# Hybrid trunk kernel: three of a pair's scatter products placed ahead of the jump out of its body, and the second expert's gather placed in the pair's block 0

## The chip, the cores and the metric

The kernel runs on one core of one Trainium2 chip. The metric is the device time of one execution in microseconds; the median of several executions is compared. The engines are PE (TensorE, matrix products), DVE (VectorE), ACT (ScalarE), POOL (GpSimd) and SP (SyncE, which issues the weight loads here).

## What is computed

Two layers of a decoder trunk with 256 tokens of width 1024 in float32. The change lies in the last sub-layer, a routed SwiGLU with eight experts of which each token takes two:

```python
def swiglu(h, w_gate_up, w_down):
    gate, up = jnp.split(h @ w_gate_up, 2, axis=-1)
    return (jax.nn.silu(gate) * up) @ w_down

def moe_swiglu(h, w_router, b_router, w_gate_up, w_down):
    tok = h.reshape(bsz * seq, d)
    probs = jax.nn.softmax(tok @ w_router + b_router, axis=-1)
    top_p, top_i = lax.top_k(probs, TOP_K)             # TOP_K = 2
    top_p = top_p / jnp.sum(top_p, axis=-1, keepdims=True)
    gates = jnp.sum(jax.nn.one_hot(top_i, N_EXPERTS) * top_p[..., None], axis=1)
    out = jnp.zeros_like(tok)
    for e in range(N_EXPERTS):                         # 8 experts, hidden width 3584
        out = out + gates[:, e:e + 1] * swiglu(tok, w_gate_up[e], w_down[e])
```

## The kernel before, in words

**Pairs.** After the router (until about 620 us) the eight experts are handled as four pairs in a loop (Fori over p, lines 2705 for PE, 1863 for DVE, 1074 for ACT). Each engine holds its own copy of the loop and, within it, five bodies, one of which is chosen at run time by the pair's kind through nested branches (expert_pairs, lines 440 to 452). A body is either wide (pair_wide: the first expert has more than 64 tokens and is computed in a split precision, with or without a further tail of 32 tokens) or light (pair_light: both experts have few tokens). In this run pairs 0, 1 and 2 are wide, 0 and 1 with a tail and 2 without one, and pair 3 is light. When a body ends, the engine jumps over the other bodies to what stands behind them, then back to the loop's head, and through the branches into the next body.

**Blocks.** An expert's hidden width is cut into seven blocks f of 512. A block needs three weight granules of 2 MB: gate, up and down. The first expert of a pair is a, the second b, and b runs one block behind a; the granules' order is that of pair_order (ag, au, ag, au, ad, bg, ad, bu, ag, ...). Each granule goes into one of seven ring buffers; SP issues the loads in order, and each waits until the granule seven places earlier was read (`used`).

**One wide block.** PE computes main_gate, main_up, main_turn (transposes of the activated product) and main_down for the 128 main tokens (24 records of 512 columns per granule, line 2227); tail_in, tail_turn and tail_down for the tail (64 records of 128 columns per granule at line 2485, 16 of 512 columns at 2497); and second_in, second_turn and second_down for expert b. ACT rounds each half of a granule (w_round, line 990), DVE forms the rest (w_rest, line 1794), and PE waits for both (`wlo_done`). DVE also multiplies the activations (lines 1800 and 1846) and writes the low part of the turned ones (a3_lo, line 1834), which releases main_down.

**A pair's end (pair_end).** PE: second_in of the last block, next_gather(p + 1) for the next pair's first expert, second_in, second_down of block 5, second_turn and second_down of block 6, and gather_second(p + 1), 32 records of 64 columns (line 2452) into T_BANK that pick the tokens of the next pair's second expert. Then comes the jump out of the body, and behind it scatter_pair, eight matmul calls at lines 2476 and 2477, each two records in the trace, that spread the pair's results over the tokens. ACT and DVE copy the results out of PSUM into ysb4 (lines 948 to 955, 1777, 1781). DVE ends with second_out(p + 1) (lines 1729 and 1733), which scales the gathered tokens of the second expert into xe2 and waits for PE's gather first. For pair 0 the gather and second_out stand ahead of the loop.

**A pair's head.** DVE forms x_lo (line 1811), splits the first halves, computes the scatter weights (weigh_pair), adds the scattered results of the pair before (add_scattered, line 1708) and copies the transposed weights (keep_pair_weights, lines 1760 and 1762), which releases main_up(0). PE's pair_weights transposes those weights into U_BANK and T_BANK; ahead of the second part it waits for `xe2_done`, since T_BANK held the gathered tokens.

## Time and profile before

| | us |
|---|---|
| median of 3 executions | 1584.27 (1583.06 to 1584.80) |
| the profiled execution's own time | 1584.35 |
| its span in the profile | 1582.6 |
| PE busy / DVE busy / ACT busy | 1407.1 / 665.0 / 499.9 |
| mean granted clock of PE | 0.94 |
| DMA, mean over the span | 300 GB/s, 410 GB/s where the queue is full |

Times in the rows are microseconds from the span's start. "issue" in a chain is time in which an engine waited for nothing that the profile shows. A bracket behind a row is the idle time of the engine just before it and what ended it. PEq, PEldq and DVEq are the sequencers, which wait, branch and load registers while their engine is idle or works off its queue.

### The profile page before, as it was taken

How to read it: one execution, taken by the hardware profiler on the slowest of the kernel's cores; microseconds unless marked ns; L12 is line 12 of the kernel's file. 1: busy time of each engine (PE TensorE's matmuls, PEld its weight loads, DVE VectorE, ACT ScalarE, POOL GpSimd, SP SyncE). 2: the span in 40 equal slices, each digit the busy share in tenths (PEclk: the TensorE clock that was granted, in tenths of full speed). 3: DMA queues.
4: the chain of work that ended last, by engine and by line, in shares of the span. 5: the costliest groups of instructions: out<-in, count | busy, mean ns of one | idle time of the engine just before them, and what ended most of it. 6: DMA issues, size and time to landing. Idle time of an engine off the chain costs nothing.

```text
span 1582.6 us, 25911 instructions
## 1 busy us (share of the span) xinstructions
PE 1407.1 (89%) x11147; PEld 995.9 (63%) x11148; DVE 665.0 (42%) x770; ACT 499.9 (32%) x562; POOL 34.8 (2%) x66
## 2 busy tenths in 40 slices
PE   4999999999998798899998899997788887796886
PEld 2763788887784547677675677675566655463443
DVE  5933445454201725755452755451664551100003
ACT  2323543433201512444432544432353431000001
POOL 2001000000100010000000000000000000000000
PEclk9989999999999996999999999999798999798898
DMA  8785875455744034399999699999599999799991
GB/s 301 274 319 207 314 287 202 173 200 176 302 160 159 1 145 174 115 368 412 411 412 410 233 368 412 410 412 410 211 353 412 412 412 409 296 413 411 413 414 75
DMA packets 206823, 474.63 MB, mean 300 GB/s; under 512 B 9986, under 2 KB 10030, under 8 KB 206670
## 3 DMA queue, kind: packets, MB, share of 16 engines
q1 hardware_dynamic: 199968, 470.83, 77.0%
q10 hardware_dynamic: 6702, 1.71, 0.5%
q8 instruction: 103, 1.69, 0.4%
q14 instruction: 50, 0.41, 0.1%
HBM read 471.47 MB, written 1.05 MB: 299 GB/s over the span
## 4 chain that ended last, share of the span: by engine, by line
PE 67%; DMA 12%; SPq 8%; issue 5%; DVE 5%; ACT 2%; DVEq 1%; ACTq 1%; POOL 0%
PE ps L2227 33%; DMA ring<-in_moe_w_down_dram 8%; SPq L488 8%; PE ps L2485 7%; PE ps L2497 5%; PE ps L2310 4%; DMA ring<-in_ada_w_dram 2%; PE ps L2374 2%; PE ps L2203 2%; PE ps L2318 2%; PE ps L2038 1%; PE ps L2452 1%; DMA ring<-in_moe_w_gate_up_dram 1%; DVE ring_lo L1794 1%; PE ps L2102 1%
## 5 line engine op out<-in xcount | busy, mean ns | idle before, releaser
L1794 DVE TENSOR_TENSOR ring_lo<-ring,w 128x2048 fp32r<-128x2048 f32 x126 | 288.3, 2289 | 177.7 <-ACT w L990 148.0
L990 ACT ACTIVATE w<-ring 128x2048 fp32r<-128x2048 f32 x126 | 240.6, 1912 | 242.4 <-PE ps L2227 241.1
L2485 PE MATMUL ps<-ring,arena 128*32 128x128 f32 (+1 forms) x5376 | 255.0, 300 | 40.1 <-DMA ring<-in_moe_w_gate_up_dram 25.6
L2485 PEld LDWEIGHTS ps<-ring,arena 128*32 128x32 f32 (+1 forms) x5376 | 191.3, 117 | 104.0 <-issue 52.1
L2227 PE MATMUL ps<-ring_lo,x_hi 128*128 128x512 f32 x560 | 220.3, 393 | 0.0
L2227 PE MATMUL ps<-w,x_hi 128*128 128x512 f32 x336 | 137.0, 408 | 16.8 <-DVE ring_lo L1794 11.8
L2227 PE MATMUL ps<-w,x_lo 128*128 128x512 f32 x336 | 132.6, 395 | 0.0
L1456 DVE TENSOR_TENSOR ring_lo<-ring,w_hi 128x2048 fp32r<-128x2048 f32 x42 | 95.6, 2290 | 86.1 <-ACT w_hi L766 86.1
L2227 PEld LDWEIGHTS ps<-ring_lo,x_hi 128*128 128x128 f32 x560 | 106.3, 190 | 21.9 <-issue 1.5
L2497 PE MATMUL ps<-ring,tri 128*32 128x512 f32 (+1 forms) x448 | 73.9, 676 | 29.7 <-DMA ring<-in_moe_w_down_dram 28.2
L766 ACT ACTIVATE w_hi<-ring 128x2048 fp32r<-128x2048 f32 x42 | 78.8, 1909 | 50.0 <-PE ps L2227 42.1
L2227 PEld LDWEIGHTS ps<-w,x_hi 128*128 128x128 f32 x336 | 64.2, 191 | 45.8 <-DVE ring_lo L1794 20.9
L2227 PE MATMUL ps<-w_hi,x_hi 128*128 128x512 f32 x224 | 89.4, 399 | 0.0
L2227 PE MATMUL ps<-w_hi,x_lo 128*128 128x512 f32 x224 | 87.4, 390 | 0.0
L2227 PE MATMUL ps<-w,a_hi 128*128 128x512 f32 x168 | 70.1, 417 | 4.5 <-DVE a_lo L1834 4.5
L2227 PEld LDWEIGHTS ps<-w,x_lo 128*128 128x128 f32 x336 | 64.2, 191 | 13.9
L2227 PE MATMUL ps<-ring_lo,a_hi 128*128 128x512 f32 x168 | 67.2, 400 | 0.0
L2227 PE MATMUL ps<-w,a_lo 128*128 128x512 f32 x168 | 67.0, 399 | 0.0
L2038 PE MATMUL ps<-ring,c 128*32 128x512 f32 x384 | 49.2, 664 | 13.3 <-DMA ring<-in_ada_w_dram 13.0
L2497 PEld LDWEIGHTS ps<-ring,tri 128*32 128x32 f32 (+1 forms) x448 | 18.7, 125 | 61.9 <-DMA ring<-in_moe_w_down_dram 31.6
L2310 PE MATMUL ps<-hT,ring 128*128 128x256 f32 x256 | 57.1, 387 | 0.0
L2497 PE MATMUL ps<-ring,arena 128*32 128x512 f32 (+1 forms) x336 | 53.2, 608 | 3.4 <-DVE arena L1708 2.7
(388 smaller groups left out, 1607.4 us busy)
## 6 DMA issues: line engine op xcount, KB each, us to landing
ring<-in_moe_w_gate_up_dram SPq DMA_DIRECT2D x112, 2048.0 KB, 16.7
ring<-in_moe_w_down_dram SPq DMA_DIRECT2D x56, 2048.0 KB, 18.2
ring<-in_ada_w_dram SPq DMA_DIRECT2D x24, 2048.0 KB, 11.0
ring<-in_ffn_w_gate_up_dram SPq DMA_DIRECT2D x14, 2048.0 KB, 12.0
ring<-in_ffn_w_down_dram SPq DMA_DIRECT2D x7, 2048.0 KB, 7.7
ring<-in_sb_w_qkv_dram SPq DMA_DIRECT2D x6, 2048.0 KB, 8.7
ring<-in_s_w_out_dram SPq DMA_DIRECT2D x2, 2048.0 KB, 8.4
ring<-in_sb_w_out_dram SPq DMA_DIRECT2D x2, 2048.0 KB, 13.4
```

What stands on the lines that cost most here:

```text
L488: sp.dma_start(dst, src).then_inc(landed[n % RING], 16)
L766: act.activation(ff_half(w_hi[:, g % 2, :], half).bitcast(F32R), ff_half(gran(ff_place(g)), half), ACT.Copy).then_inc(whi_done, 1)
L990: act.activation(half3(h).bitcast(F32R), ff_half(gran(pair_place(*main_granule(n))), half), ACT.Copy).then_inc(whi_done, 1)
L1456: dve.tensor_tensor(ff_half(ring_lo[(ff_place(g)) % RING][:, :], half).bitcast(F32R), w, ff_half(w_hi[:, g % 2, :], half), ALU.subtract).t ...
L1794: dve.tensor_tensor(ff_half(ring_lo[place % RING][:, :], half).bitcast(F32R), ff_half(gran(place), half), half3(h), ALU.subtract).then_inc ...
L2038: ins = pe.matmul(ps[32 * j:32 * j + 32, ada_bank(i), :], c32[:, 4 * part_k + k, :], gran8(places[r])[:, 4 * part_k + k, :], start=k == 0, ...
L2203: ins = pe.matmul(ps[:, 2 * i + half, :], yT[:, k, P * tt:P * tt + P], gran4(WOUT_PLACES[half])[:, k, 512 * n:512 * n + 512], start=k == 0 ...
L2227: ins = pe.matmul(dst, stationary[a].bitcast(F32R), moving[b].bitcast(F32R), start=start and i == 0, stop=stop and i == 2)
L2310: ins = pe.matmul(ps[:, 2 * (r % 2) + j // 2, 256 * (j % 2):256 * (j % 2) + 256], gran8(n)[:, k, P * j:P * j + P], hT[:, k, :], start=k == ...
L2318: ins = pe.matmul(ps[:, Y_BANK + 2 * tt + r, :], tokens(k, tt), gran8(n)[:, k, :], start=k == 0, stop=k == KD - 1)
L2485: ins = pe.matmul(dst[width * r:width * r + width, 0:cols], x[:, k, 0:width], weights[:, k, cols * r:cols * r + cols], start=k == 0, stop= ...
L2497: ins = pe.matmul(ps[width * r:width * r + width, bank, :], a[:, j, 0:width], weights[:, j, 512 * h:512 * h + 512], start=first and i == 0 ...
```

## The change

Three of the eight calls of scatter_pair, those of the first expert's results for the outputs 0, 1 and 2, go into a new function scatter_first, which PE runs at the end of pair_end, ahead of the jump; they wait for the copies into ysb4 through two new semaphores, first_act and first_dve. The other five calls stay behind the jump. In a light pair one of ACT's copies moves to DVE, so that both semaphores are counted in either kind. gather_second(p) leaves pair_end and the place ahead of the loop; it now stands in block 0 of its own pair, behind main_up(0) (in the light body behind the first up product), and waits for the second `st_done` of that pair. second_out(p) moves on DVE into block 0 too, behind a3_lo (light: behind the first product_first). pair_weights no longer waits for `xe2_done`; the first second_in does.

```diff
--- before.py
+++ after.py
@@ -321,6 +321,7 @@
         xe1_ps, xe1_done = sem("xe1_ps"), sem("xe1_done")
         pick2_done, onehot2_done, xe2_ps, xe2_scaled, xe2_done = (
             sem("pick2_done"), sem("onehot2_done"), sem("xe2_ps"), sem("xe2_scaled"), sem("xe2_done"))
+        first_act, first_dve = sem("first_act"), sem("first_dve")
         n_silu, n_act, n_tr, n_aT = sem("n_silu"), sem("n_act"), sem("n_tr"), sem("n_aT")
 
 
@@ -946,8 +947,8 @@
                 wait_used2(act, p, "ad", FB - 1)
                 if not light:
                     act.activation(ysb4[:, 0, :], ps[:, Y_BANK, :], ACT.Copy)
-                act.activation(ysb4[0:64, 2, :], ps[0:64, Y_BANK + 2, :], ACT.Copy)
-                act.activation(ysb4[64:P, 3, :], ps[64:P, Y_BANK + 2, :], ACT.Copy)
+                    act.activation(ysb4[64:P, 3, :], ps[64:P, Y_BANK + 2, :], ACT.Copy)
+                act.activation(ysb4[0:64, 2, :], ps[0:64, Y_BANK + 2, :], ACT.Copy).then_inc(first_act, 1)
 
             def second_results(p):
 
@@ -1774,12 +1775,14 @@
                 second_selection(p + 1)
                 if not light:
                     wait_used2(dve, p, "ad", FB - 1)
-                    dve.tensor_copy(ysb4[:, 1, :], ps[:, Y_BANK + 1, :])
+                    dve.tensor_copy(ysb4[:, 1, :], ps[:, Y_BANK + 1, :]).then_inc(first_dve, 1)
+                else:
+                    wait_used2(dve, p, "ad", FB - 1)
+                    dve.tensor_copy(ysb4[64:P, 3, :], ps[64:P, Y_BANK + 2, :]).then_inc(first_dve, 1)
                 next_out(p + 1)
                 product_second(p, FB - 1, width)
                 wait_used2(dve, p, "bd", FB - 1)
                 dve.tensor_copy(ysb4[0:64, 3, :], ps[0:64, Y_BANK + 3, :]).then_inc(ysb_dve, 1)
-                second_out(p + 1)
 
             def pair_wide(p, tails, split, tail, width):
 
@@ -1833,6 +1836,8 @@
                     dve.wait_ge(a3_done, split * FB + f + 1)
                     dve.tensor_tensor(a3_lo[:, :, :].rearrange("p k n -> p (k n)").bitcast(F32R), ps[:, G_BANK, :],
                                       a3_hi[:, :, :].rearrange("p k n -> p (k n)"), ALU.subtract).then_inc(m_aT, 1)
+                    if f == 0:
+                        second_out(p)
                     if f < FB - 1:
                         w_rest(2 * n + 6)
                         w_rest(2 * n + 7)
@@ -1852,6 +1857,8 @@
                 keep_pair_weights(p)
                 for f in range(FB):
                     product_first(f)
+                    if f == 0:
+                        second_out(p)
                     if f:
                         product_second(p, f - 1, W2)
                 pair_end(p, W2, True)
@@ -1859,7 +1866,6 @@
             with dve.If(paired(dve) > 0):
                 dve.memset(rt[:, 0, 72:73], 0.0).then_inc(sc_done, 4 * PAIRS)
                 second_selection(0)
-                second_out(0)
                 with nc.Fori(0, PAIRS, engines=[dve.engine], hint_back_edge=True) as p:
                     tails, split, by_kind = expert_pairs(dve, p)
                     by_kind(lambda tail, width: pair_wide(p, tails, split, tail, width), lambda: pair_light(p))
@@ -2447,6 +2453,7 @@
             def gather_second(p):
 
                 pe.wait_ge(onehot2_done, 2 * p + 2)
+                pe.wait_ge(st_done, 2 * p + 3)
                 for k in range(KD):
                     for tt in range(TT):
                         ins = pe.matmul(ps[:, T_BANK, W2 * k:W2 * k + W2], hn[:, tt, P * k:P * k + P], g2[:, tt, :],
@@ -2461,21 +2468,33 @@
                         ins = pe.transpose(ps[:, U_BANK, 256 * i + P * tt:256 * i + P * tt + P],
                                            gw2[:, tt, P * i:P * i + P], ident[:, :])
                 ins.then_inc(st_ps, 1)
-                pe.wait_ge(xe2_done, p + 1)
                 for tt in range(TT):
                     ins = pe.transpose(ps[:, T_BANK, P * tt:P * tt + P], gw2[:, tt, 2 * P:3 * P], ident[:, :])
                 ins.then_inc(st_ps, 1)
 
+            def scattered(i):
+
+                tt, h = divmod(i, 2)
+                return ps[:, Y_BANK + i, :], slice(P * tt, P * tt + P), h
+
+            def scatter_first(p):
+
+                pe.wait_ge(first_act, p + 1)
+                pe.wait_ge(first_dve, p + 1)
+                for i in range(3):
+                    dst, tokens_t, h = scattered(i)
+                    pe.matmul(dst, scT[:, 0, tokens_t], ysb4[:, h, :], start=True, stop=False)
+
             def scatter_pair(p):
 
                 pe.wait_ge(ysb_act, p + 2)
                 pe.wait_ge(ysb_dve, p + 2)
                 for i in range(4):
-                    tt, h = divmod(i, 2)
-                    tokens_t = slice(P * tt, P * tt + P)
-                    pe.matmul(ps[:, Y_BANK + i, :], scT[:, 0, tokens_t], ysb4[:, h, :], start=True, stop=False)
-                    pe.matmul(ps[:, Y_BANK + i, :], (scT2 if h else scT[:, 1, :])[:, tokens_t], ysb4[:, 2 + h, :],
-                              start=False, stop=True).then_inc(sc_ps, 1)
+                    dst, tokens_t, h = scattered(i)
+                    if i == 3:
+                        pe.matmul(dst, scT[:, 0, tokens_t], ysb4[:, h, :], start=True, stop=False)
+                    pe.matmul(dst, (scT2 if h else scT[:, 1, :])[:, tokens_t], ysb4[:, 2 + h, :], start=False, stop=True
+                              ).then_inc(sc_ps, 1)
 
             def shared(dst, x, weights, width):
 
@@ -2514,7 +2533,7 @@
                 elif b:
                     pe.wait_ge(n_aT, p * FB + b)
                 else:
-                    pe.wait_ge(st_done, 2 * p + 3)
+                    pe.wait_ge(xe2_done, p + 1)
                 at = 4 * W2 if what == "bu" else 0
                 shared(ps[:, T_BANK, at:at + 4 * W2], xe2, gran8(n), width).then_inc(used[n % RING], 1)
 
@@ -2538,7 +2557,7 @@
                 second_down(p, FB - 2, width)
                 second_turn(p, FB - 1, width)
                 second_down(p, FB - 1, width)
-                gather_second(p + 1)
+                scatter_first(p)
 
             def pair_wide(p, tails, split, tail, width):
 
@@ -2641,6 +2660,8 @@
                         pair_weights(p)
                     tail_down(f)
                     main_up(f)
+                    if f == 0:
+                        gather_second(p)
                     if f:
                         second_in(p, "bu", f - 1, width)
                     main_turn(f)
@@ -2685,6 +2706,8 @@
                 pair_weights(p)
                 for f in range(FB):
                     first_in("au", f)
+                    if f == 0:
+                        gather_second(p)
                     if f:
                         second_in(p, "bg", f - 1, W2)
                     first_turn(f)
@@ -2701,7 +2724,6 @@
 
             with pe.If(paired(pe) > 0):
                 pe.transpose(ps[:, T_BANK, 0:P], ident[:, :], ident[:, :]).then_inc(sc_ps, 4 * PAIRS)
-                gather_second(0)
                 with nc.Fori(0, PAIRS, engines=[pe.engine], hint_back_edge=True) as p:
                     tails, split, by_kind = expert_pairs(pe, p)
                     by_kind(lambda tail, width: pair_wide(p, tails, split, tail, width), lambda: pair_light(p))
```

## Rows read from the trace of the kernel before

**Rows 1.** The page's second part: DMA engines' busy tenths in 40 slices of the span.

```profile
DMA  8785875455744034399999699999599999799991
```

**Rows 2.** Stages: us, busy time of each engine, granted clock, DMA share, GB/s.

```profile
620.00:631.00 11.00, 9.88 (x96) 9.58 (x96) 1.99 (x7) 4.33 (x9) 0.00 (x0) 0.53 0.85 312
...
884.00:894.00 10.00, 8.88 (x95) 7.08 (x96) 6.18 (x6) 4.48 (x4) 0.00 (x0) 1.00 0.67 237
...
1124.50:1136.00 11.50, 8.26 (x29) 6.28 (x30) 6.14 (x6) 4.31 (x3) 0.00 (x0) 0.84 0.62 221
```

**Rows 3.** Chain that ended last, passage from pair 1 to 2: start, us, what.

```profile
1086.10 3.73 PE ps L2452 x32
...
1090.68 5.69 issue
...
1096.52 4.84 issue
...
1103.74 5.89 issue
...
1124.62 7.36 PE ps L2227 x24
```

**Rows 4.** The branch at the end of a body, line 440, window 849 to 857.

```profile
L440 PEldq COMPARE_BRANCH  x1: 5935/5935/5935, 850.8 to 850.8; - x1
```

**Rows 5.** Chain, passage from pair 0 to 1 and block 0 of pair 1.

```profile
847.30 1.92 PE ps L2497 x16
...
852.94 4.04 issue
...
867.97 1.98 PE ps L2485 x62
...
883.95 5.73 PE ps L2227 x24
...
893.32 5.73 PE ps L2227 x24
```

**Rows 6.** DVE in order of time, same passage; the bracket is idle time before.

```profile
866.70 1.29 DVE L1811 TENSOR_TENSOR x_lo<-arena,x_hi 128x512 fp32r<-128x512 f32 x2 [12.31 <-issue]
...
869.98 2.29 DVE L1794 TENSOR_TENSOR ring_lo<-ring,w 128x2048 fp32r<-128x2048 f32 x1 [1.98 <-PE ps L2485]
...
872.60 2.28 DVE L1794 TENSOR_TENSOR ring_lo<-ring,w 128x2048 fp32r<-128x2048 f32 x1
```

**Rows 7.** Groups by line, from 900 us on: busy, mean ns.

```profile
L2612 PE MATMUL ps<-ident,arena 128*128 128x128 f32 x52 | 8.5, 286 | 0.8 <-DVE arena L1800 0.8
...
L1031 ACT ACTIVATE a_hi<-ps 128x512 fp32r<-128x512 f32 x13 | 7.8, 598 | 41.5 <-PE ps L2612 41.5
...
L1834 DVE TENSOR_TENSOR a_lo<-ps,a_hi 128x512 fp32r<-128x512 f32 x13 | 9.0, 691 | 0.1
```

**Rows 8.** In order of time, entry of pair 0, DVE and PE.

```profile
628.13 3.13 PE L2485 MATMUL ps<-ring,arena 128*32 128x128 f32 x64
...
631.61 1.29 DVE L1811 TENSOR_TENSOR x_lo<-arena,x_hi 128x512 fp32r<-128x512 f32 x2 [1.95 <-issue]
...
635.22 2.28 DVE L1794 TENSOR_TENSOR ring_lo<-ring,w 128x2048 fp32r<-128x2048 f32 x1
```

**Rows 9.** Chain, block 0 of pair 3 (the light one).

```profile
1362.08 6.53 PE ps L2485 x32
...
1370.22 3.65 PE ps L2497 x16
```

**Rows 10.** Tail of the kernel: DVE in order of time, then the chain.

```profile
1568.68 1.22 DVE L1260 TENSOR_TENSOR tbuf<-ident,gate_c 128x1024 f32<-128x1024 f32 x1
...
1557.16 3.72 PE ps L2452 x32
...
1571.35 1.73 PE ps L2070 x4
...
1573.18 1.24 DVE gg L1269
```

## The prediction

> **What bounds the kernel.** I read the page's slices first. The DMA engines stand at 9 or 10 tenths for most of the second half of the span [rows 1]: the expert weights stream without a break, except for a dip at the head of each pair. The stage table shows those dips: 0.67 and 0.62 of the DMA engines' time in block 0 of pairs 1 and 2 [rows 2]. The ring holds seven granules, so at the head of a pair the loads run until the ring is full and then wait until TensorE has read the first granules. In the middle of a pair a microsecond saved on an engine is lost again behind the loads. At the head it is kept, because it moves the moment from which the loads run without a gap, and everything after that moves with it. So I ask of each of the five passages (into pair 0, three between pairs, out of the last) how much earlier its head gets going.
>
> Next the chain of waits. Between pairs 1 and 2 it leaves PE after the second expert's gather (3.73 us) and then runs on DVE through three stretches without work, 5.69, 4.84 and 5.89 us, ahead of the first instruction of the next body; PE's main_up starts only at 1124.62 [rows 3]. Between pairs 0 and 1 it lies on PE: second_down from 847.30, the gather, 4.04 us of nothing, the scatter, the first tail products [rows 5]. DVE idles 12.31 us there and its first split then waits 1.98 us for PE's tail product [rows 6]. PE's branch out of the body takes 5.94 us from 850.8 on; PE idles only 4.04 of it because some 18 records already stand in its queue when the sequencer reaches the branch [rows 4, 5].
>
> On a branch the Trainium skill speaks twice. Advanced Engine Details and Errata, Control Flow Timing, gives about 108 ns for a compare-and-branch; the 5.94 us here contradict that as a price for this jump. Runtime: NRT & Kernel Launch, Instruction fetch mechanics, says that a taken branch whose target is not in the current window waits for a fetch, and the trace agrees. By the first the jumps would be worth nothing; the 5.94 us rule it out, and I build no rival on it.
>
> **Part by part. The price in block 0.** Each pair now gathers its second expert between main_up(0) and main_turn(0). In pair 1 main_up(0) starts at 883.95 and takes 5.73; main_down(0) starts at 893.32 [rows 5], so 3.64 us lie between and DVE fills them. With the gather the sequence is 3.73 (gather) + 0.65 (four transposes, 8.5 us over 13 blocks) + 0.60 (ACT a_hi) + 0.69 (DVE a_lo) [rows 3, 7] and about 0.15 of hand-overs: 5.8. The cost is 5.8 - 3.64 = **2.2 us** in each wide pair; bounds 0 (if it hid) and 3.73. second_out adds some 1.4 us to DVE behind a_lo. The next split is wanted only after main_down(0), 5.73 us later, and takes 2.28, so 2 us of cover remain; I cost it at nothing, and at 1.4 if that cover is gone. In the light pair 1.6 us lie between the up product's end at 1368.61 and the down product at 1370.22 [rows 9], 1.1 of them the turn and its eviction, which stay behind the gather; so there it costs 3.73 + 1.1 - 1.6 = 3.2.
>
> **DVE's gain.** It no longer waits for the gather and its eviction before it branches. At the second passage it would branch behind L1781, which starts as PE ends at 1086.10, plus 0.16; it does so now at 1090.68 [rows 3]: **4.4 us**. The fetches behind it stay.
>
> **PE's gain.** A call of the scatter is two records of 0.43 us at full clock (four records take 1.73 [rows 10]). The three calls ahead of the jump are 2.6 us, in which PE works while its sequencer is already in the branch. With a look-ahead of 18 records, the 16 of second_down and the six let the branch start once four or five of second_down have gone, near 847.7 instead of 850.8: **3.1 us**. The remaining five calls take 4.3 us at full clock or 8.6 at half, against the 10 us that pass now from the end of the 4.04 us stretch, at 856.98, to the next body. But PE goes on only when its own branches are through, so its gain at the next body is the same 3.1 us and not the removed products.
>
> **Passage into pair 0.** Gather and second_out fall away before the loop. DVE's x_lo starts at 631.61, 1.95 us after second_out's last instruction; without it DVE is ready near 623.5. PE's tail gate product is at 628.13 and takes 3.13 at half clock (0.53 granted [rows 2]); it can start near 622.8 (an estimate: the loop's register loads behind the router, a little longer than DVE's 1.95 us). Gate 626.0, tail up 629.5, second split (w_rest(1)) near 629.8, against 635.22 [rows 8]: 5.4. If the clock rises sooner it is 6.4. Less the 2.2: **3.6**, bounds 2.5 and 4.3.
>
> **Passage into pair 1** (a tail, so PE's entry counts). The bulk of the tail gate product, 62 of 64, starts at 867.97, after a stall with no releaser [rows 5], which I read as code still being fetched behind the jump; so it comes 3.1 earlier, at 864.9. PE has had 2 to 6 us without work by then. At half clock the 62 take 3.3 us and the tail gate ends at 868.2 instead of 869.98 [rows 6], 1.8 earlier, and the tail up product loses another 0.6; at full clock the gain stays 3.1. I take w_rest(1) (now 872.60 [rows 6]) 1.7 earlier; from there DVE's own queue carries the chain to main_up(0). 1.7 - 2.2 = **-0.5**, a loss; bounds -2.2 and +1.2.
>
> **Passage into pair 2** (no tail, DVE's chain throughout). 4.4 - 2.2 = 2.2. In block 0 of this pair the granted clock is 0.84 [rows 2], with main_up(0) at 7.36 us instead of 5.73 [rows 3, 5], and PE is idle for 3.2 of the 11.5 us [rows 2], most of it ahead of main_down(0). The gather fills most of that, so one of the two falls of the clock should go, some 1.0: **3.2**, bounds 1.5 and 4.5.
>
> **Passage into pair 3** (light). DVE's four fetches start 4.4 earlier and its chain releases the up product at 1362.08, which runs at half clock (6.53 us); then the gather. The first down product (1370.22 [rows 9]) comes 4.4 - 3.2 = 1.2 earlier, with a little for the clock **1.5**, bounds 0 and 2.5.
>
> **Out of the last pair.** No gather, no second_out, so DVE's tbuf (1568.68 + 1.22) is ready 4.4 earlier, at 1565.46. PE works through the sixteen scatter records without a break, from second_down's end at 1557.16 [rows 10] to 1564.0, and then has no work for 1.5 us, which I take to be too short for the clock to fall. The four L2070 records then take 1.73 and DVE's four adds behind tbuf (2.4 us) end last: gg starts near 1567.9 instead of 1573.18 [rows 10]. **5.2**, bounds 4.1 (half clock at L2070) and 5.3. No load runs here; all of it is kept.
>
> **Sum.** 3.6 - 0.5 + 3.2 + 1.5 + 5.2 = 13.0 us. The profiled execution took 1584.35 us (its span 1582.6), which stands 0.08 above the median of 1584.27. 1584.35 - 13.0 = 1571.35, as a median **1571.3 us**. The bounds of the terms add up to 5.9 and 17.8 us, so 1566.5 to 1578.4.
>
> **Rivals.** (a) The gather costs block 0 its full 3.73 us in the wide pairs and 3.73 in the light one, since something other than DVE fills the 3.64 us gap, and the clock gives nothing back. Start 1.7, pair 1 -2.0, pair 2 0.7, pair 3 0.7, end 5.2: 6.3 us, **1578.0**. Against it: the chain in that gap is DVE's a_lo. (b) The clock favours it: full clock at the tail products and at L2070, 4.3 + 1.2 + 4.5 + 2.5 + 5.3 = 17.8, **1566.5**. For it: the falls come after idle stretches that all shift. Against: those stretches do not get shorter. (c) It does not do what it says: the branch starts only when PE's queue has drained, or the loads' dips are filled by something else. Then only the end is kept and the block costs cancel the rest: within 3 us, **about 1582**. Against: the branch starts 2.1 us before the gather ends [rows 4, 5]. (d) **Slower**: block 0's code on PE grows by the gather, 32 records and their weight loads, behind a jump whose first page is exhausted at once (the wait ahead of the row at 867.97). If that moves a page boundary so that a fetch of 4.9 us (the middle of the stretches in rows 3) stands open in every one of the four block 0s, it costs 19.6: 1584.3 - 13.0 + 19.6 = **1590.9**. It decides from three open fetches on. Against: main_up's 24 products last 5.7 us and cover a fetch.
>
> The Trainium skill (Runtime: NRT & Kernel Launch, Instruction fetch mechanics) has pages of 256 instructions fetched in sequence; by it rival (d) can happen, and no run here shows where the boundaries will lie.
>
> **Chances.** The forecast 0.66, (a) 0.13, (b) 0.09, (c) 0.06, (d) 0.06. The forecast's own bounds take in (a) and (b), so I give 1566.5 to 1578.5; outside lie (c) and (d). Some 0.2% (3.2 us) is what a measurement of this kernel can tell from no change; the forecast, (a) and (b) lie beyond it, (c) within: faster 0.87, same 0.07, slower 0.06.
>
> **What would show it.** In the profile after: DVE's idle time ahead of x_lo stays near 12.3 us at the first passage and starts 4.4 earlier; PE's line-440 branch lasts 5.9 us and starts before the six records do; ten scatter records after it instead of sixteen; 32 gather records between main_up(0) and main_turn(0), and 5.8 us instead of 3.6 from the end of main_up(0) to main_down(0); DMA share in block 0 up in pair 2, not in pair 1; gg about 5 us nearer to the last second_down. A gap in block 0 with no releaser behind the gather, or xe2 waited for in block 1, would make the prediction wrong.

## The result

| kernel | median, us | ratio to before (95% interval) |
|---|---|---|
| before | 1583.66 | |
| after | 1568.64 (1567.70 to 1572.38) | 0.9911 (0.9897 to 0.9925) |
| after, measured again | 1570.13 (1567.10 to 1571.43); before beside it 1583.93 | 0.9918 (0.9905 to 0.9932) |

The change takes about 14 to 15 us off. The profiled execution of after took 1568.50 us (span 1566.7); 1571.3 was forecast.

**How the two profiles are compared.** I cut the routed part at five marks that both kernels have: the first DVE instruction behind the router's selection (line 1620, after 1621), and the start of the last second_down of each pair (line 2497, after 2516); the last cut is the start of the last DVE instruction. "To down(0)" is the time from such a mark to the next pair's main_down(0), or to the light pair's first down product.

| | before | after | gain | to down(0), before | after |
|---|---|---|---|---|---|
| mark to the last second_down of pair 0 | 238.0 | 234.4 | 3.6 | 47.3 | 43.5 |
| pair 1 | 236.9 | 237.7 | -0.8 | 46.0 | 46.9 |
| pair 2 | 239.7 | 235.3 | 4.4 | 51.6 | 47.1 |
| pair 3 | 229.6 | 227.2 | 2.4 | 46.3 | 44.3 |
| to the end | 24.7 | 20.0 | 4.7 | | |
| sum | 969.0 | 954.6 | 14.4 | | |

The other 1.6 us between the profiles lie ahead of the first mark (609.27 against 607.69), where nothing was changed. In fourteen profiles of twelve kernels that mark lay anywhere from 605.99 to 611.68, so I count it as chance.

**The jump.** PE's branch out of the body of pair 0 (answers to [rows 4]), one line of after, one of experiment e1 (below):

```profile
L441 PEldq COMPARE_BRANCH  x1: 5890/5890/5890, 842.4 to 842.4; - x1
```

```profile
L441 PEldq COMPARE_BRANCH  x1: 5890/5890/5890, 845.5 to 845.5; - x1
```

In after it begins 0.24 us behind the start of second_down (842.11), in before 3.48 behind it (850.78, [rows 4, 5]). What PE then does, PE in order of time in after; a bracket is the idle time ahead (this answers to [rows 5]):

```profile
842.11 1.92 PE L2516 MATMUL ps<-ring,tri 128*32 128x512 f32 x16 [0.46 <-ACT tri L977]
843.96 2.84 PE L2486 MATMUL ps<-arena 128*128 128x512 f32 x6
848.50 2.81 PE L2496 MATMUL ps<-arena 128*128 128x512 f32 x6 [1.70 <-issue]
...
856.81 1.42 PE L2504 MATMUL ps<-ring,arena 128*32 128x128 f32 x34 [3.78 <-issue]
859.48 1.93 PE L2504 MATMUL ps<-ring,arena 128*32 128x128 f32 x30 [1.25 <-issue]
861.79 3.31 PE L2504 MATMUL ps<-ring,arena 128*32 128x128 f32 x64 [0.39 <-ACT arena L1005]
...
873.93 2.77 PE L2516 MATMUL ps<-ring,arena 128*32 128x512 f32 x16 [2.36 <-DVE arena L1709]
```

Six scatter records run while the branch is open, and PE still stands idle twice, for 1.70 and 3.78 us. DVE in the same passage (answers to [rows 6]):

```profile
857.28 1.29 DVE L1814 TENSOR_TENSOR x_lo<-arena,x_hi 128x512 fp32r<-128x512 f32 x2 [12.51 <-issue]
```

x_lo comes 15.2 us behind the start of second_down instead of 19.4.

**Block 0 and the end.** The chain of after, block 0 of pair 1, block 0 of pair 2 and of the light pair, and the end (answers to [rows 3, 5, 9, 10]):

```profile
876.81 6.43 PE ps L2233 x24
883.25 3.52 PE ps L2459 x32
886.76 0.44 PE ps L2631 x4
887.21 1.88 PE ps L2504 x64
889.09 5.67 PE ps L2233 x24
```

```profile
1115.62 5.75 PE ps L2233 x24
1121.37 3.52 PE ps L2459 x32
...
1126.00 0.70 DVE a_lo L1837
```

```profile
1349.54 5.24 PE ps L2504 x32
1354.77 3.71 PE ps L2459 x32
...
1359.38 3.65 PE ps L2516 x16
```

```profile
1546.08 3.70 issue
...
1550.02 3.29 issue
...
1554.72 2.48 DVE arena L1709 x4
...
1557.23 1.23 DVE gg L1270
```

The gather stands between main_up(0) and main_turn(0). From main_up(0)'s end to main_down(0) it is 5.78 us in pair 1 (883.24 to 889.02 by PE in order of time; the chain puts main_down(0) at 889.09, where the product before it ends); 1121.37 to 1126.93, 5.56, in pair 2; and 1354.77 to 1359.38, 4.61, in the light pair. At the end DVE goes from its two fetches straight into tbuf and the four adds, and the copy to gg begins 14.9 us behind the last second_down instead of 19.7. PE's L2076 runs at full clock (four records from 1554.86 to 1556.84) and is not waited for.

Stages of after (columns as in [rows 2]): the entry of pair 0, the tail products of pair 1, block 0 of pair 1 and of pair 2:

```profile
616.00:627.00 11.00, 7.29 (x139) 6.39 (x142) 6.24 (x17) 7.34 (x14) 0.00 (x0) 0.69 0.60 219
857.50:865.00 7.50, 5.86 (x112) 4.52 (x102) 3.36 (x3) 3.54 (x3) 0.00 (x0) 0.54 1.03 408
879.50:889.50 10.00, 10.00 (x119) 8.95 (x118) 4.48 (x5) 4.17 (x3) 0.00 (x0) 1.00 0.67 247
1115.50:1127.00 11.50, 9.78 (x61) 8.58 (x61) 6.41 (x6) 3.54 (x3) 0.00 (x0) 1.00 0.84 308
```

As forecast, the DMA share of block 0 rose in pair 2 (0.62 to 0.84) and not in pair 1 (0.67 in both). The clock of pair 2's block 0 is 1.00 instead of 0.84, but that of the tail products was 0.54 in pair 1 (1.2 GHz most of the time), where it was 1.00 in before.

### The profile page after: what moved, and what is told of

It is laid out like the page before. It is cut to its first block, busy times and chain, and to the rows that moved or that the text cites. A ratio compares the mean times of both kernels' runs of the same rounds, so it can differ in the third digit from the quotient of the medians.

```text
span 1566.7 us, 25857 instructions
## 1 busy us (share of the span) xinstructions
PE 1391.6 (89%) x11115; PEld 986.4 (63%) x11116; DVE 664.2 (42%) x769; ACT 499.8 (32%) x561; POOL 35.2 (2%) x66
## 4 chain that ended last, share of the span: by engine, by line
PE 70%; DMA 11%; SPq 7%; issue 6%; DVE 4%; ACT 2%; ACTq 1%; DVEq 0%; POOL 0%
PE ps L2233 34%; PE ps L2504 9%; SPq L489 7%; DMA ring<-in_moe_w_down_dram 7%; PE ps L2516 6%; PE ps L2316 4%; DMA ring<-in_ada_w_dram 2%; PE ps L2380 2%; PE ps L2044 2%; PE ps L2209 2%; PE ps L2324 2%; PE ps L2449 1%; DMA ring<-in_moe_w_gate_up_dram 1%; PE ps L2459 1%; DVE arena L1222 1%
## 5 line engine op out<-in xcount | busy, mean ns | idle before, releaser
L991 ACT ACTIVATE w<-ring 128x2048 fp32r<-128x2048 f32 x126 | 240.6, 1912 | 233.7 <-PE ps L2233 232.0
L2233 PE MATMUL ps<-w,x_hi 128*128 128x512 f32 x336 | 137.1, 408 | 15.8 <-DVE ring_lo L1797 13.7
```

Of the source, the lines that this page charges most:

```text
L991: act.activation(half3(h).bitcast(F32R), ff_half(gran(pair_place(*main_granule(n))), half), ACT.Copy).then_inc(whi_done, 1)
L2233: ins = pe.matmul(dst, stationary[a].bitcast(F32R), moving[b].bitcast(F32R), start=start and i == 0, stop=stop and i == 2)
```

## The experiments

All are compared by the same cuts. The pieces of a line are those of one profiled execution; the medians are of 4 to 10. A profiled execution can lie well off its kernel's median (e1: 1570.59 us against 1565.45; e3: 1576.46 against 1579.40; after again: 1567.10 against 1570.13), so the kernels are ranked by the medians and not by the sums.

| kernel | median | ratio (95%) | pair 0 | pair 1 | pair 2 | pair 3 | end | sum |
|---|---|---|---|---|---|---|---|---|
| before | 1583.6 to 1583.9 | | 238.0 | 236.9 | 239.7 | 229.6 | 24.7 | 969.0 |
| after | 1568.64 | 0.9911 (0.9897-0.9925) | 234.4 | 237.7 | 235.3 | 227.2 | 20.0 | 954.6 |
| after again | 1570.13 | 0.9918 (0.9905-0.9932) | 233.4 | 238.1 | 235.5 | 227.0 | 19.7 | 953.8 |
| e1, gather alone | 1565.45 | 0.9874 (0.9850-0.9897) | 234.1 | 235.5 | 235.3 | 229.0 | 20.0 | 953.9 |
| e1 again | 1566.17 | 0.9895 (0.9878-0.9912) | 233.6 | 235.4 | 234.8 | 227.0 | 20.3 | 951.2 |
| e2, scatter alone | 1590.16 | 1.0043 (1.0025-1.0062) | 237.4 | 245.9 | 238.8 | 227.7 | 24.1 | 973.8 |
| e8, e2 with shifted code | 1581.76 | 0.9988 (0.9974-1.0002) | 234.7 | 236.3 | 238.6 | 231.9 | 24.4 | 965.9 |
| e3, second_out alone | 1579.40 | 0.9973 (0.9962-0.9984) | 238.2 | 238.5 | 237.4 | 223.9 | 26.1 | 964.0 |
| e4, short gather | 1560.92 | 0.9858 (0.9825-0.9892) | 232.0 | 232.8 | 235.7 | 224.0 | 19.6 | 944.0 |
| e7, scatter twice | 1571.64 | 0.9919 (0.9902-0.9937) | 234.2 | 236.2 | 237.0 | 227.2 | 20.2 | 954.8 |
| e10, after with shifted code | 1568.89 | 0.9910 (0.9882-0.9939) | 233.0 | 237.0 | 235.2 | 228.8 | 19.9 | 953.8 |
| e5, gather in head, pairs 2, 3 | 1567.10 | 0.9895 (0.9876-0.9913) | 234.3 | 237.7 | 235.6 | 225.7 | 21.7 | 955.0 |
| e6, e5 and e1 | 1563.54 | 0.9872 (0.9857-0.9887) | 234.3 | 235.2 | 235.3 | 226.1 | 19.6 | 950.5 |
| e9, gather in all heads, and e1 | **1560.06** | **0.9854 (0.9821-0.9887)** | 231.7 | 233.0 | 235.0 | 224.1 | 20.5 | 944.3 |

### Which half of the change carries the gain: e1 and e2

e1 takes scatter_first out of the changed kernel:

```diff
                 second_down(p, FB - 1, width)
-                scatter_first(p)
...
-                    if i == 3:
-                        pe.matmul(dst, scT[:, 0, tokens_t], ysb4[:, h, :], start=True, stop=False)
+                    pe.matmul(dst, scT[:, 0, tokens_t], ysb4[:, h, :], start=True, stop=False)
```

> The changed kernel with all sixteen scatter records behind the jump again; the gather and second_out stay in block 0. My theory: what brings PE and DVE to the jump earlier is the gather and second_out leaving the pair's end; PE's entry into the next body is set by its own branches and fetches, and the six records ahead of the jump only fill time in which PE has nothing else to do. Then this kernel takes 0 to 1 us longer than the changed one, 1568.6 to 1569.6. The rival: the products ahead of the jump carry a part, since ten records behind it are done sooner than sixteen; the three passages with a next body and the end then each lose 1 to 2.6 us, 1573 to 1579.

Measured: 1565.45 us, not above the changed kernel but some 3 us below. e1's branch begins 0.12 us behind second_down, 0.14 in its second profile (845.47 against 845.33; the second of the two branch lines above). So six records of the scatter are not needed for the early branch; the gather's leaving does it. The pieces of pair 1 showed where the surprise lay, and I ran it again beside the changed kernel:

> The changed kernel itself, once more, on the same chip as the others of this group. It tells how much of a difference of a few us lies in the phase of the router's end and of the clock: the router's end lay anywhere from 605.99 to 610.55 us in five kernels whose code is the same up to there. If that is chance: 1564 to 1569 us, with the same passages within 1 us. If the changed kernel's 1568.6 us were fixed by its code: within 0.5 us of it.

> All sixteen scatter records behind the jump, once more beside the changed kernel. In its first profile PE's tail products of pair 1 ran at full clock and without a stall, and the passage into pair 1 was 2.2 us shorter than in the changed kernel, the one into pair 3 1.8 us longer. If both repeat, it stands within 1 us of the changed kernel; if only the first is due to the code and the second to the clock's phase, 1 to 3 us below it; if the six records ahead of the jump help after all, above it by 1 us or more.

Measured: 1570.13 against 1566.17. The changed kernel's passages came again within 1.0 us, though its median lies in neither of the two ranges that I had given. The 2.2 us of pair 1 came again (2.7), pair 3's 1.8 did not (0.0). The two intervals just overlap; what carries the difference is that it came three times, here, in the first pair of runs and between e5 and e6 below (3.6 us), each time with some 2.5 us in pair 1. PE in e1 again, in order of time:

```profile
845.33 1.92 PE L2515 MATMUL ps<-ring,tri 128*32 128x512 f32 x16 [0.46 <-ACT tri L977]
851.62 2.04 PE L2494 MATMUL ps<-arena 128*128 128x512 f32 x2 [4.36 <-issue]
853.46 1.63 PE L2495 MATMUL ps<-arena 128*128 128x512 f32 x2
...
860.16 1.28 PE L2503 MATMUL ps<-ring,arena 128*32 128x128 f32 x34
862.67 1.07 PE L2503 MATMUL ps<-ring,arena 128*32 128x128 f32 x30 [1.23 <-issue]
864.13 1.95 PE L2503 MATMUL ps<-ring,arena 128*32 128x128 f32 x64 [0.39 <-ACT arena L1005]
```

and its stage with the tail products:

```profile
860.00:866.20 6.20, 4.52 (x130) 3.56 (x129) 3.58 (x3) 2.40 (x3) 0.00 (x0) 1.00 1.05 411
```

All sixteen records run without a break right up to the tail products, and these then take 1.07 and 1.95 us at full clock, where after takes 1.93 and 3.31 at half. The clock falls in e1 too, but sooner: 5.9 us behind second_down's start (5.6 in the first profile), so that it is the first scatter records that run at half clock (2.04 us for two instead of 1.02), and these have time to spare. In after it falls 15.7 us behind (16.2 in the second profile), on the tail products, which have none. DVE's w_rest(1) starts 21.0 to 21.1 us behind second_down in the four profiles with sixteen records behind the jump (e1 twice, e6, e9) and 23.2 to 23.7 in four of the five with ten; the fifth is e4, at 21.4, where the clock fell 14.6 us behind second_down and was back for the tail up product. So ten records behind the jump mostly bring the fall to the tail products, but not always.

> The changed kernel with the six records of the first three products done twice: once ahead of the jump, and again, as part of all sixteen, behind it. It holds the work ahead of the jump of the one and the work behind it of the other. If the work behind the jump is what keeps PE's clock up for the tail products of pair 1, the passage into pair 1 is that of the kernel with all sixteen behind: 44.6 us from second_down to main_down(0), not 46.9. If it is the place of the code (or the start of the branch) and not the work, 46 to 48. The time is within 2 us of the changed kernel in either case.

e7 does the six records in both places (the first time with stop=True, so that each product is complete, and then again as part of all sixteen). Its tail gate product ran at full clock like e1's, but the clock fell at 865.1, within the tail up product, and pair 1 took 236.2, with 45.3 us to main_down(0): between the two. So the work behind the jump brings back 1.6 of the 2.3 us. The time, 1571.64 us, is 3.0 and 1.5 above the two medians of after, where I had allowed 2.

e2 is the other half: the gather and second_out at the pair's end as in before, scatter_first behind the gather (its place in pair_end, against after):

```diff
                 second_down(p, FB - 1, width)
+                gather_second(p + 1)
                 scatter_first(p)
```

> The other half alone: the gather and second_out stand at the pair's end as before, and the six scatter records behind the gather, still ahead of the jump. My theory: DVE's way to its branches is unchanged and PE's grows by up to 2.6 us of products, of which the sequencer sees little; the time is that of the kernel before within 1 us, 1582.5 to 1584.5. The rival, that the products ahead of the jump carry the gain: 1572 to 1579.

Measured: 1590.16 us, slower than before by 0.4%, outside what either theory allowed. Nine microseconds are lost in pair 1. PE in e2 in order of time, behind the six scatter records (the last line is from the passage into pair 2):

```profile
855.48 3.59 PE L2494 MATMUL ps<-arena 128*128 128x512 f32 x5 [2.06 <-issue]
860.65 1.22 PE L2494 MATMUL ps<-arena 128*128 128x512 f32 x1 [1.58 <-issue]
...
869.70 0.63 PE L2502 MATMUL ps<-ring,arena 128*32 128x128 f32 x2 [4.42 <-issue]
872.19 3.63 PE L2502 MATMUL ps<-ring,arena 128*32 128x128 f32 x62 [1.85 <-issue]
...
1106.71 0.70 PE L2494 MATMUL ps<-arena 128*128 128x512 f32 x1 [1.51 <-issue]
```

PE stops in the middle of the scatter with no releaser, behind the same record in all three passages between pairs (1.58, 1.51 and 1.86 us), and the loop's branch behind it begins late; in the first passage:

```profile
L2723 PEldq COMPARE_BRANCH  x1: 5972/5972/5972, 860.8 to 860.8; - x1
```

e8 is e2 with 20 transposes (each one record and one weight load) ahead of the loop on PE, which only move the code behind them:

```diff
+            for _ in range(20):
+                pe.transpose(ps[:, T_BANK, 0:P], ident[:, :], ident[:, :])
             with pe.If(paired(pe) > 0):
```

> The kernel with the gather at the pair's end and the six scatter records ahead of the jump, its PE code behind the router shifted by 20 transposes (40 instructions), which run while PE waits for the router. Unshifted, it took 9.0 us more than the kernel before in the passage into pair 1: in the middle of the ten scatter records behind the jump PE stopped for 1.6 us with no releaser, and the branch to the loop's head began at 860.76, 5.5 us after the first jump's end and not 0.3. If that is a fetch of code at a page boundary in the scatter, the shift moves it and the passage falls from 55 to 49 to 51 us; the time to 1584 to 1587. If it is a wait (a copy of ACT's or DVE's), the passage stays at 55 us and the time at 1590.

```profile
855.13 2.81 PE L2494 MATMUL ps<-arena 128*128 128x512 f32 x6 [2.03 <-issue]
...
863.46 3.59 PE L2502 MATMUL ps<-ring,arena 128*32 128x128 f32 x64 [3.80 <-issue]
```

```profile
L2725 PEldq COMPARE_BRANCH  x1: 5205/5205/5205, 855.3 to 855.3; - x1
```

The stop is gone, the branch begins 0.4 us behind the first jump's end, and pair 1 takes 236.3 us instead of 245.9. So the stop came from where the code lies, as a fetch of code does, and its price was the late branch behind it, the half clock that followed, and a second stop (1.85 us) in the next body: 9.6 us, where I had expected 4 to 6 of the shift. In the passages into pairs 2 and 3 the loop's branch came as late (15.8 us behind second_down, where before has 9.9), and the pairs took 238.8 and 227.7 us, no more than in before: there PE's entry does not set the time. With that accident out of the way, the scatter half of the change stands at 0.9988 (0.9974 to 1.0002), and this median is still flattered: the transposes kept PE's clock at 1.00 through the entry of pair 0, where pair 0 gained 2.7 us on e2. Half clock took 4.2 us back in pair 3: PE had waited 2.7 us for a load ahead of the last second_down, and the gather behind it took 7.1 us instead of 3.8.

### What the gather costs in block 0: e4

In the changed kernel the gather is cut from 32 records to 4.

```diff
             def gather_second(p):
...
-                for k in range(KD):
+                for k in range(1):
```

> The changed kernel with the second expert's gather cut from 32 records to 4 (one of eight column groups; the rest of the second expert's tokens is left out of the computation). It prices the gather in block 0. By my sum a wide pair's gap from main_up(0) to main_down(0) falls back from 5.8 to 3.64 us, filled by DVE: 1.9 to 2.2 us in each of three wide pairs and 2.8 to 3.2 in the light one, 8.5 to 9.8 us, about 1560. By rival (a), the gather's full price, 3.3 us in each of four pairs, 13 us, about 1556. By the loads as the bound from pair 2 on, the last two pairs give less: 6 to 7 us, about 1562.

Measured: 1560.92 us; 7.7 and 9.2 us below the two medians of after. The gaps are as forecast: in pair 1 main_down(0) starts 3.64 us behind main_up(0)'s end, with DVE in the chain again,

```profile
874.50 5.75 PE ps L2233 x24
...
880.87 1.51 DVE ring_lo L1797
...
883.07 0.70 DVE a_lo L1837
883.89 0.49 PE ps L2233
```

against 5.78 in after. But the pieces are not 2.2, 2.2, 2.2 and 3.2. They are 1.4 to 2.4, 4.9 to 5.4, nothing, and 3.1 to 3.2. In pair 1 the gap gave 2.1 us, and the rest lies ahead of it, in code that both kernels share: main_gate(0) starts 1.9 us sooner, behind tail products that ran partly at full clock, then tail_down at 1.92 us instead of 2.77, main_up(0) at 5.75 instead of 6.43. That is the clock's phase in this profile and not the gather's price. In pair 2 the gap shrank by 1.8 us, but main_up(0) ahead of it ran at half clock (8.33 us instead of 5.75), and so did main_down(0) behind it (7.31 us), as it did in after. The sum was right, its division was not.

### DVE's part alone: e3

```diff
                 dve.tensor_copy(ysb4[0:64, 3, :], ps[0:64, Y_BANK + 3, :]).then_inc(ysb_dve, 1)
-                second_out(p + 1)
...
                 w_rest(1)
+                second_out(p)
```

> The kernel before with one move: DVE's second_out leaves the pair's end for the head of the next body (behind w_rest(1), light: ahead of the scatter weights). The gather stays at the pair's end, so PE's way is as before; only DVE branches 4.4 us sooner, and its head grows by the 1.4 us of second_out. If DVE's chain decides passages 2 and 3 and PE's passage 1: 0 to -1.4 us in passage 1, +3.0 in passages 2 and 3 each, nothing to 3 us at the end, in all 5 to 8 us, 1575.5 to 1579. The rival, that PE's late entry decides everywhere: no gain and 1.4 us lost for each of three heads, 1584 to 1588.

Measured: 1579.40 us, 4.2 below before: just short of the range of the first theory, and well below the rival. By pieces, of a profile 2.9 us below the median: pair 1 -1.6 (DVE's head is longer and PE is no earlier), pair 2 +2.3, pair 3 +5.8, end -1.3, where 3.0 was expected in each of pairs 2 and 3. So DVE's early branch is worth something by itself where there is no tail, as claimed. At the end it is worth nothing as long as PE keeps the gather; DVE in order of time:

```profile
1555.16 1.23 DVE L1260 TENSOR_TENSOR tbuf<-ident,gate_c 128x1024 f32<-128x1024 f32 x1
1557.22 0.69 DVE L1708 TENSOR_TENSOR arena<-arena,ps 128x512 f32<-128x512 f32 x1 [0.83 <-PE ps L2477]
1560.06 0.69 DVE L1708 TENSOR_TENSOR arena<-arena,ps 128x512 f32<-128x512 f32 x1 [2.15 <-PE ps L2477]
```

The adds now wait for PE's scatter. In after and in e1 they do not, so the 4.7 us at the end need the gather gone from PE as well as second_out from DVE, and not scatter_first.

### Where code pages lie: e10

> The changed kernel with its PE code behind the router shifted by the same 20 transposes. It tests rival (d): how much the place of the page boundaries is worth in the changed kernel. In its passage into pair 1 PE does 34 of the tail gate's 64 records, stops for 1.3 us and goes on 5.6 us after the end of the loop branch. If that stop is a code fetch, the number of records ahead of it changes with the shift (by 20 records), while the time at which PE goes on stays 5.6 us behind the branch; the kernel's time is within 2 us of the changed kernel's. If a boundary falls into the scatter or into block 0, 3 to 5 us more in a passage.

Measured: 1568.89 us. PE in order of time:

```profile
856.77 1.08 PE L2504 MATMUL ps<-ring,arena 128*32 128x128 f32 x14 [3.82 <-issue]
859.45 3.13 PE L2504 MATMUL ps<-ring,arena 128*32 128x128 f32 x50 [1.60 <-issue]
```

Fourteen records ahead of the stop instead of 34: the boundary moved by the 20 records inserted. The time at which PE goes on did not: 859.45 is 5.63 us behind the end of the loop's branch (848.57 and 5.25). The same distance is 5.65 in before (with two records ahead of the stop), 5.64 and 5.63 in the profiles of after, 5.64 in e1 again, 5.65 in e9 and 5.63 in e7; in e2, e3, e4 and e5 it is 5.45 to 5.57. In the first profile of e1 and in e6, whose tail gate product began 4.6 to 4.7 us behind the branch's end, PE did not stop at all. The kernel's time is that of the changed kernel, as expected.

### A place for the gather that costs less: e5, e6, e9

e5 moves the gather in the bodies without a tail into the head, behind the gate's tail product or its like; the second part of the transposed weights, which needs the same bank, is formed behind the first down product.

```diff
                 tail_in("ag", 0, TAIL_GATE, t_gate)
+                if not tail:
+                    gather_second(p, True)
...
                     main_down(f)
+                    if f == 0 and not tail:
+                        pair_weights_rest(p, True)
```

> The changed kernel, but in the body without a tail (pair 2) and in the light one (pair 3) the gather stands in the body's head, in which PE waits for DVE's fetches anyway, and the second part of the transposed scatter weights is formed behind the first down product. My theory: the block-0 price of the gather (5.6 instead of 3.6 us in pair 2, 4.6 instead of 1.6 in pair 3) goes: 5 us, 1563.6, plus or minus 1 for the clock. The rivals: the gap in block 0 is kept by other steps (the copy of the transposed weights moves ahead of a_lo or main_down), so 1566 to 1568; or the time is won only to be lost to the weight loads, which can't be had sooner, in the next block, 1568.6.

Measured: 1567.10 us. Pair 3 gained 1.5 of the 3 us, pair 2 nothing, and the end lost 1.7, since L2084 fell into half clock (four records in 3.69 us and not 1.98). The forecast of 1563.6 was wrong. The gap in pair 2's block 0 did fall, from 5.56 to 3.77 us, but both products around it now ran at half clock (7.35 and 7.36 us).

> Both moves together: in the bodies of pairs 2 and 3 the gather stands in the head, and all sixteen scatter records stand behind the jump. From the profiles so far: U to the second_down of pair 0 234.2, then 235.5, 235.4, 225.7 to 227, and 20 to 21.7 us to the end, together 951 to 953.5 against 954.6 in the changed kernel: 1 to 3.5 us below it. The rival, that the loads set the time of pairs 2 and 3 anyway: no difference from the kernel with the one move alone, that is 0 to 1 us below.

e6 adds e1's edit: 1563.54 us, 3.6 below e5; the sum of its pieces is 4.1 below the changed kernel's, where I had expected 1 to 3.5.

e9 puts the gather in the bodies with a tail, too, between pair_weights and tail_down:

```diff
-                        pair_weights(p, not tail)
+                        pair_weights(p, True)
+                        if tail:
+                            gather_second(p, True)
                     tail_down(f)
```

There too the second part of the transposed weights now stands behind the first down product.

> The kernel with the gather in the heads of pairs 2 and 3 and all sixteen scatter records behind the jump, with one more move: in the bodies with a tail too (pairs 0 and 1) the gather goes into the head, between pair_weights and tail_down, where PE waits 2.2 us. There it costs 3.7 less 2.2, 1.5 us, against 2.2 in block 0: 0.7 us gained in each of pairs 0 and 1, 1562.2 in all. The rival: tail_down and main_up(0) are late anyway by 1.5 us and DVE's copies come behind: no gain, or up to 1.5 us lost in each.

Measured: **1560.06 us**, 23.5 us below before on the same chip, and 8.6 to 10.1 below the two medians of after: the fastest complete kernel of the case. Pairs 0 and 1 gained 2.6 and 2.2 us each over e6, not 0.7. PE in e6 and then in e9, in order of time:

```profile
872.85 3.54 PE L2531 MATMUL ps<-ring,arena 128*32 128x512 f32 x16 [2.21 <-DVE arena L1709]
```

```profile
866.12 3.68 PE L2468 MATMUL ps<-arena,hn 128*128 128x64 f32 x32
869.74 1.92 PE L2531 MATMUL ps<-ring,arena 128*32 128x512 f32 x16
```

The gather fills the 2.21 us, and tail_down behind it runs at full clock, 1.92 us instead of 3.54. I had priced the idle time and not the clock that it costs: 2.2 us off block 0, less 1.5 for the gather, and 1.6 for the clock make 2.3. The 1.6 are not there every time: in the twenty-four passages into pairs 0 and 1, over all kernels but e9, in which PE waited 2.0 to 2.4 us ahead of tail_down, it ran wholly or partly at half clock in seventeen and at full clock in seven.

## Why the prediction was right, and where it was not

**The bound.** Right, and the runs show it. The jumps and their fetches set the passages, and what a head gains is kept because the loads start sooner. In each head SP issues four loads of gate and up weights as ring buffers come free; SP in order of time in pair 2, before and then after:

```profile
1121.78 34.82 SPq L488 DMA_DIRECT2D ring<-in_moe_w_gate_up_dram  x4
```

```profile
1113.13 34.64 SPq L489 DMA_DIRECT2D ring<-in_moe_w_gate_up_dram  x4
```

The fourth is out at 1156.60 and at 1147.77, 72.4 and 68.0 us behind the mark, and the pair's last second_down starts 167.3 us later in both. This distance is 167.0 to 167.8 us in pairs 0, 1 and 2 of all fourteen profiles, while these pairs took 231.7 to 245.9 us, and 171.3 to 172.9 in pair 3. A pair's time is the time at which its fourth load goes out and a constant.

**The price in block 0.** The size was right, 5.78 and 5.56 us against 5.8 in the wide pairs, 4.6 us against 4.8 (1.6 and 3.2) in the light one. In pairs 0 and 1 the reason was not, and the agreement there is luck: behind the gather, tail_in's 64 records (1.88 us) carry PE up to main_down(0), and a_lo is done by then. As a cost to the kernel it was some 2 us in pairs 0 and 1 and 3 us in the light pair (e4). In pair 2, where I charged 2.2, neither e4 nor the gather in the head (e5, e6, e9) gained anything: seven kernels with the early branch, whatever the place and length of their gather, take 234.8 to 235.7 us there (e7, at 237.0, is the exception). Block 0 of pair 2, us from PE in order of time:

| | main_up(0) | gap | main_down(0) | sum |
|---|---|---|---|---|
| before | 7.35 | 3.77 | 7.34 | 18.5 |
| after | 5.75 | 5.56 | 7.31 | 18.6 |
| e1 | 7.36 | 5.56 | 5.74 | 18.7 |
| e5 | 7.35 | 3.77 | 7.36 | 18.5 |
| e9 | 7.38 | 3.77 | 7.31 | 18.5 |

At full clock either product takes 5.7 us. Of the six profiles with the full gather in this block, five (after and e1 twice, e10) have one of the two products at half clock and the sixth, e7, has both; the four without it (e4, e5, e6, e9) have both. So what the gather adds to the gap, 1.8 us, comes back as one fall of the clock less, 1.6 us. That the gather is what spares the fall is read off these profiles and was not tested by itself.

**DVE's gain,** forecast 4.4: measured 4.2 in pair 1 and 4.6 in pair 2 (x_lo 21.1 us behind second_down instead of 25.7). Right.

**PE's gain,** forecast 3.1: the branch begins 3.24 us sooner against second_down. Right. All of it is the gather's leaving: e1 gives 3.36 without scatter_first. The step put the removed products at nothing for PE's entry, which is so, but it put their price at nothing too, and they cost 3 to 4 us (e1 twice, e6 against e5).

**Pair 0,** forecast 3.6: 3.6, and 4.6 in the second profile. PE entered at 621.16, which with the 1.6 us of the mark is 622.7 on before's time; 622.8 was my estimate. The clock was 0.69 there, so the rise that would have given one more microsecond came late.

**Pair 1,** forecast -0.5: -0.8 and -1.2. I had w_rest(1) 1.7 us earlier, since half clock at the tail products would take back the rest of the 3.1; it came 2.0 earlier (23.3 us behind second_down instead of 25.3). What I did not see is that the change itself brings the fall there: e1, with the same early branch, has full clock there, w_rest(1) comes 4.2 earlier, and the pair gains 1.4 to 1.5 us.

**Pair 2,** forecast 3.2: 4.4 and 4.2. The mechanism was right and all three sizes were off to the same side: main_up(0) starts 4.6 us sooner behind the mark (forecast 4.4), the gap grew by 1.8 (2.2), and the two products around it lost 1.6 by one fall of the clock less, which I had put at 1.0. I had expected the fall ahead of main_down(0) to go; in after it stayed (1127.46 onwards) and the one in main_up(0) went, in e1 it was the other way round, with the same sum.

**Pair 3,** forecast 1.5: 2.4 and 2.6. The clock in the up product gave 1.3 (5.24 us instead of 6.53) where I allowed 0.3. With the gather cut the pair takes 224.0 us (e4), with the gather in the head 224.1 to 226.1 (e9, e5, e6), and in e3, where it stands at the pair's end, 223.9.

**The end,** forecast 5.2: 4.7 and 5.1. tbuf came 3.9 us sooner behind the last second_down (11.3 us instead of 15.2), not 4.4. Full clock in the four records (L2076) was right. In e5 they fell into half clock, the case of my lower bound of 4.1, and the end gained 3.0.

**The rivals.** (a), the full price, is refuted in block 0's gaps. (b) did not come as a whole, though its clock gains in pairs 2 and 3 did. (c) falls with PE's branch, which begins 0.24 us behind second_down's start and not when the queue has drained. (d), a page boundary that moves, did not happen in the changed kernel, but its mechanism is real. Its price is not the one figure per place that I gave it: e2 has the same stop in three passages, and it cost 9 us in the first and nothing in the other two. The Trainium skill (Runtime: NRT & Kernel Launch, Instruction fetch mechanics) has code fetched in pages of 256 instructions. The traces agree that a boundary is fixed to a place in the code: 20 records and 20 weight loads inserted ahead moved it by 20 records.

## What to carry to other kernels

Ahead of a jump, take away what delays the branch; work put there to fill the time gains nothing where the engine's own fetches decide, and moving it there can shift a fall of TensorE's clock onto products that have no time to spare. Price idle time of PE together with the products around it, since they may run at half clock. Find the load from which the weights stream again in each stage, and measure a change by how far it moves that load. When a small edit of code costs several microseconds in one passage, shift the code by a few instructions before believing the edit.

## What the runs showed of the hardware that I had not expected

- A stop of PE in the body behind a jump ended 5.63 to 5.65 us after the loop branch's end in seven profiles, however many records came before it (34, 14 or 2), and 5.45 to 5.57 us after it in four more.
- One stop for code in the scatter, 1.58 us of idle time on PE, delayed the branch behind it by 5.1 us (it began 5.5 us behind the first jump's end instead of 0.4) and cost the passage into pair 1 9 us. The same stop cost nothing in the passages into pairs 2 and 3.
- 2.0 to 2.4 us of idle time ahead of tail_down were followed by half clock in seventeen of twenty-four cases (3.54 us for 1.92 in e6) and by full clock in seven; 64-column gather records in their place kept it at full clock in both pairs of e9. The two idle stretches of the changed kernel (1.70 and 3.78 us, with ten scatter records between them) were followed by 0.54 in the tail products; nearly the same two in e4 (1.70 and 3.83) by full clock in the tail up product.
- Once the fourth load of a head is out, the rest of the pair takes the same time within 0.8 us in pairs 0 to 2, whatever the engines do in the head.
- The mark behind the router varied by 5.7 us between profiles of kernels that are the same up to there. Differences of 2 us between two such kernels need either several profiles or cuts that leave this part out.
